# The first search of a gathered layer in two parts, one head after the other

## The chip, the cores and the metric

The kernel runs on one core of one Trainium2 chip. The core has five engines with a queue each: TensorE (PE, matrix products), VectorE (DVE), ScalarE (ACT), GpSimd (POOL) and SyncE (SP), and 16 DMA engines that move data between HBM and the on-chip memory SBUF. PE writes to PSUM. The metric is the device time of one execution in microseconds (us), the median of several.

## What is computed

A model of several layers on 256 tokens of 1024 numbers each, all in float32. The part that matters here is the second kind of feed-forward layer, which occurs twice (stages `peer0` and `peer1`). Each token picks 16 experts for each of 8 heads out of 16384 by product keys, and every expert is one row of `u` and one of `v`:

```python
def peer_ffn(h, w_q, sub_keys, u, v):
    q = (ht @ w_q).reshape(T, PEER_HEADS, 2, PEER_QDIM // 2)
    s = jnp.einsum('thpd,pnd->thpn', q, sub_keys)
    top_s, top_i = lax.top_k(s, PEER_TOPK)
    cand_s = top_s[:, :, 0, :, None] + top_s[:, :, 1, None, :]
    cand_i = top_i[:, :, 0, :, None] * PEER_NKEYS + top_i[:, :, 1, None, :]
    best_s, best_j = lax.top_k(cand_s.reshape(T, PEER_HEADS, -1), PEER_TOPK)
    experts = jnp.take_along_axis(cand_i.reshape(T, PEER_HEADS, -1), best_j, axis=-1)
    gates = jax.nn.softmax(best_s, axis=-1)
    act = jax.nn.gelu(jnp.einsum('cd,ced->ce', xc, u[ec]))
    return jnp.einsum('ce,ced->cd', gc * act, v[ec])
```

## The kernel before

**Gathers.** The 256 tokens lie in two tiles of 128, and 8 heads by 16 picks make 128 picks a token, so a layer needs 256 gathers. Gather m fetches for each of 128 tokens the row of u and v of its pick m: 128 rows of 8 KB, 1.05 MB. POOL issues them in order of m (line 686) into a ring of 8 slots (`RING`). Gather m from 8 on first waits until PE has used the slot of m - 8 (`v_used`), and each unit of 32 gathers (`UNIT`) waits for its picks (`experts_made`). A unit is two heads of one tile.

**What is done with a gather.** DVE makes a dot product of the u rows with the tokens (line 1982). For every two gathers (`BATCH`) ACT makes the gelu (line 943), DVE makes two diagonal matrices from gelu and gate (`weights`, line 1971), and PE weighs the v rows with them (`weigh`, line 1427), which frees the slot.

**Before the first gather.** The queries are h times w_q, in four groups of 512 columns (four query blocks of 128, that is two heads). Group 0 is projected at once (`project`, line 987), ACT copies it from PSUM (`take`, line 743), PE scores it against the keys (`key_scores`, line 1387), ACT copies the scores (`copy_keys`, line 917), and DVE searches the two heads (`search(0)`): sixteen largest of 128 for each of four query blocks (lines 1861 to 1877), the 256 sums of each head (1887), sixteen largest of those (1894 to 1910), and the expert numbers from them (1915 to 1944). Then the gates (lines 1948 to 1959, with an exponential on ACT, line 923). Meanwhile PE turns the tokens back to rows (`turn_tok`, line 1376, copied by `copy_tok`, line 910), projects group 1 at once and makes its scores. Only then is PE ready to weigh, and ACT, whose queue holds `take` of group 1, `take_row` and `copy_keys(1)` ahead of the first gelu, ready for that. Groups 2 and 3 are projected between the weighings, two products behind each of gathers 0 to 15 and 26 to 41 (`project_step`, line 1400). The search of each later unit is spread over the gathers of the unit before it, one step behind each dot product from the fourth on.

**Order.** Each engine runs its own queue in the order written, and semaphores tie them. SP loads the weight groups into three slots, each when the group three before it has been projected (line 521): the last w_q group behind projection 0, the odd layer's weights behind the later projections. Nothing else moves while the gathers run.

## Time and profile before

| | us |
|---|---|
| median of 3 runs | 2480.36 |
| lowest and highest | 2479.7 and 2483.38 |
| the profiled execution, its own time | 2479.74 |
| its span | 2477.9 |
| PE busy | 1919.7 (77%) |
| DVE busy | 1354.5 (55%) |
| POOL busy | 552.8 (22%) |
| ACT busy | 323.3 (13%) |

The profile is of one execution. Times in the rows are counted from the start of its span. The first gathered layer runs from about 883 us to 1580, the second from 1770 to the end. In a timeline row the numbers are the start and the duration of a group of like instructions, and the brackets give the idle time of the engine before it and who ended it. PE has two records for each product of 256 or 512 columns, so `x64` is 32 products. PEld is PE's loading of the stationary operand. DMA share is the mean busy share of the 16 DMA engines.

### The profile page before, as it was taken

To read this page: it belongs to the slowest core of one execution; us is meant where nothing else is said; L and a number is where in the kernel's file an instruction comes from.
4 is the path that set the end of the run, shared out by engine and by line. 5 is a ranking of instruction groups with operands and counts; after the bars stand their busy time and mean duration, and the time that the engine had idled before them with its cause. 6 is when DMAs were issued, how large, how long until landed. Compare 5 with 4: busy or idle time off the path is not lost. (4 is left out here: it accounts for less than half of the span.)

```text
span 2477.9 us, 24089 instructions
## 1 busy us (share of the span) xinstructions
PE 1919.7 (77%) x8926; PEld 1027.1 (41%) x8926; DVE 1354.5 (55%) x3221; ACT 323.3 (13%) x795; POOL 552.8 (22%) x563
## 2 busy tenths in 40 slices
PE   6998666666589688977777777788889877777776
PEld 4666333333266464532222222374565322232222
DVE  2623000010167537767877786555177788678765
ACT  1052000000111321000000000203211100000000
POOL 1000000000000004344343433100034434444432
PEclk9998888888789799999999999999999999999999
DMA  9987999999698039999999999693289999999997
GB/s 381 409 259 289 428 428 431 430 428 429 282 374 327 11 124 419 419 419 421 421 415 421 413 420 421 272 370 115 81 328 421 421 421 421 412 414 421 414 422 292
DMA packets 145523, 894.76 MB, mean 361 GB/s; under 512 B 17305, under 2 KB 29433, under 8 KB 62457
## 3 DMA queue, kind: packets, MB, share of 16 engines
q0 software_dynamic: 73728, 536.90, 52.3%
q1 hardware_dynamic: 71672, 356.25, 36.1%
q8 instruction: 75, 1.23, 0.2%
q14 instruction: 48, 0.39, 0.0%
HBM read 889.68 MB, written 3.42 MB: 360 GB/s over the span
## 5 line engine op out<-in xcount | busy, mean ns | idle before, releaser
L1427 PE MATMUL psum<-sb_area 128*128 128x512 f32 x2048 | 974.4, 619 | 286.3 <-DVE sb_area L1971 283.5
L1982 DVE CUSTOM_DVE_ANT_0 sb_area<-sb_area 128x1024 f32<-128x1024 f32 x512 | 627.2, 1225 | 305.3 <-DMA sb_area<-in_peer_uv,sb_peer_e 303.2
L686 POOL DMA_INDIRECT sb_area<-in_peer_uv,sb_peer_e x512 | 542.2, 1059 | 1123.0 <-PE psum L1427 721.7
L1427 PEld LDWEIGHTS psum<-sb_area 128*128 128x128 f32 x2048 | 382.6, 195 | 835.1 <-DVE sb_area L1971 454.1
L1171 PE MATMUL psum<-sb_area 128*32 128x256 f32 x2048 | 173.6, 514 | 134.4 <-DMA sb_area<-in_moe_w_gu 132.4
L987 PE MATMUL psum<-sb_area 128*128 128x256 f32 x1040 | 235.1, 388 | 5.1 <-ACT sb_area L730 3.5
L1626 DVE COPY sb_area<-psum 128x128 f32<-128x128 f32 x32 | 9.3, 292 | 397.0 <-PE psum L1181 397.0
L987 PEld LDWEIGHTS psum<-sb_area 128*128 128x128 f32 x1040 | 202.0, 195 | 39.1 <-issue 5.1
L943 ACT ACTIVATE sb_small<-sb_small 128x2 f32<-128x2 f32 x256 | 52.1, 204 | 1201.7 <-DVE sb_small L1982 1201.7
L1971 DVE SCALAR_TENSOR_TENSOR sb_area<-sb_ident,sb_small,sb_area 128x128 f32<-128x128 f32 x512 | 156.1, 346 | 44.9 <-ACT sb_small L943 40.4
L1171 PEld LDWEIGHTS psum<-sb_area 128*32 128x32 f32 x2048 | 83.5, 146 | 224.2 <-DMA sb_area<-in_moe_w_gu 145.9
L992 PE MATMUL psum<-sb_area 128*128 128x512 f32 (+1 forms) x392 | 165.2, 581 | 11.9 <-DVE sb_area L1839 10.3
L1540 DVE SCALAR_TENSOR_TENSOR sb_area<-sb_area,sb_c_silu 128x2048 f32<-128x2048 f32 x56 | 131.7, 2351 | 74.6 <-DMA sb_area<-in_ada_w 71.5
L674 POOL TENSOR_SCALAR_AFFINE_SELECT sb_area<-sb_area 128x256 f32<-128x256 f32 x1 | 0.4, 408 | 767.0 <-DVE sb_area L1808 767.0
L992 PEld LDWEIGHTS psum<-sb_area 128*128 128x128 f32 x392 | 74.4, 192 | 98.7 <-issue 84.8
L1400 PE MATMUL psum<-sb_area 128*128 128x256 f32 x256 | 66.6, 383 | 0.0
L1194 PE MATMUL psum<-sb_area 128*32 128x256 f32 x1024 | 61.9, 381 | 4.6 <-DVE sb_area L1626 4.6
L1400 PEld LDWEIGHTS psum<-sb_area 128*128 128x128 f32 x256 | 49.1, 193 | 33.9 <-issue 30.5
L1514 DVE TENSOR_TENSOR sb_area<-psum,sb_row 128x512 f32<-128x512 f32 x12 | 8.3, 692 | 79.7 <-PE psum L992 79.7
L806 ACT ACTIVATE sb_area<-psum 128x128 f32<-128x128 f32 x32 | 8.9, 278 | 294.6 <-PE psum L1171 294.6
L1016 PE MATMUL psum<-sb_ident,sb_area 128*128 128x128 f32 x96 | 19.9, 393 | 34.9 <-DVE sb_area L1488 34.9
L743 ACT ACTIVATE sb_area<-psum 128x1024 f32<-128x1024 f32 x21 | 21.4, 1021 | 188.9 <-PE psum L987 188.9
(276 smaller groups left out, 1331.6 us busy)
## 6 DMA issues: line engine op xcount, KB each, us to landing
sb_area<-in_moe_w_gu SPq DMA_DIRECT2D x32, 4096.0 KB, 33.8
sb_area<-in_ada_w SPq DMA_DIRECT2D x72, 1024.0 KB, 12.9
sb_area<-in_moe_w_dn SPq DMA_DIRECT2D x32, 2048.0 KB, 24.4
sb_area<-in_peer_w_q SPq DMA_DIRECT2D x8, 2048.0 KB, 8.1
sb_area<-in_sb_w_in SPq DMA_DIRECT2D x6, 2048.0 KB, 21.7
sb_area<-in_odd_w_in SPq DMA_DIRECT2D x6, 2048.0 KB, 13.2
sb_area<-in_even_w_in SPq DMA_DIRECT2D x5, 2048.0 KB, 17.9
sb_area<-in_peer_uv,sb_peer_e POOLq DMA_INDIRECT x512, 13.0
```

The costliest lines, as they stand in the source:

```text
L686: pool.indirect_dma_start(uv_rows[s], None, rows, bass.IndirectOffsetOnAxis(ap=peer_e[:, m:m + 1], axis=0)).then_inc(named(f"uv_loaded{s}" ...
L743: act.activation(g["dst"], src, ACT.Copy, scale=g["scale"]).then_inc(proj_out, 1)
L943: act.activation(gelu[:, cols], dots[:, cols], ACT.Gelu_apprx_tanh).then_inc(named("gelu_done"), 1)
L987: last = pe.matmul(ps[:, b + f // 2, (f % 2) * T:(f % 2 + 1) * T], w[:, k, f * P:(f + 1) * P], src[:, k, :], start=(k == 0), stop=(k == nk ...
L992: last = pe.matmul(ps[:, b + t, 0:cols], src[:, k, t * P:(t + 1) * P], w[:, k, 0:cols], start=(k == 0), stop=(k == nk - 1))
L1171: last = pe.matmul(ps[SLOTS * q:SLOTS * (q + 1), 6 + e % 2, 0:2 * FQ], xe[e // QUAD % 2][:, k, SLOTS * (e % QUAD):SLOTS * (e % QUAD + 1)], ...
L1194: last = pe.matmul(ps[SLOTS * q:SLOTS * (q + 1), 6 + b, 0:DQ], turned_act[b][:, SLOTS * f:SLOTS * (f + 1)], moe_dn[e % EXPERT_BUFS][:, f, ...
L1400: last = pe.matmul(ps[:, b + f // 2, (f % 2) * T:(f % 2 + 1) * T], wring[n % 3][:, k, f * P:(f + 1) * P], hT[:, k, :], start=(k == 0), sto ...
L1427: last = pe.matmul(ps[:, 4 + 2 * t + half, :], diag[:, s, :], uv_rows[s][:, D + half * HALF:D + (half + 1) * HALF], start=(k == 0), stop=( ...
L1540: dve.scalar_tensor_tensor(acc, ring[slot], c, acc, ALU.mult, ALU.add).then_inc(ada_used, 1)
L1971: last = dve.scalar_tensor_tensor(diag[:, m % RING, :], ident[:, :], gelu[:, m % BODY:m % BODY + 1], g.broadcast_to([P, P]), ALU.mult, ALU ...
L1982: dve.tensor_tensor_reduce(uv_rows[s][:, 0:D], uv_rows[s][:, 0:D], h_tok[:, m // P, :], 1.0, 0.0, ALU.mult, ALU.add, dots[:, m % BODY:m % ...
```

## The change

The first unit of each gathered layer is split by head. PE makes the first two query blocks of group 0 (16 products), signals `head_projected`, makes three products of the third block, scores the first head on token tile 0, turns part of the tokens, and then makes the other 13 products and the scores of the second head. ACT copies the first two blocks and the first head's scores on their own, and the rest behind them. DVE runs the search for head 0 alone, then for head 1, and makes the gates of both behind that. POOL starts gather 0 when head 0's picks are there, and waits once more before gather 16 (`PEER_K`). All counts of the semaphores `keys_copied`, `key_scored` and `experts_made` get one more a layer. Later units are searched as before, two heads at a time. In the diff the rest of `find_picks` only replaces the fixed sizes by `count`, `nq` and `nk`.

```diff
@@ -441,6 +441,16 @@
 
         def layer_of(stage):
             return int(stage[-1])
+
+        KEY_PARTS = 2 * NT * 2 + 1
+
+        def keys_at(L, i, t):
+
+            return KEY_PARTS * L + NT * i + t + 2
+
+        def experts_at(L, m):
+
+            return (UNITS + 1) * L + (m // UNIT + 2 if m >= UNIT else m // PEER_K + 1)
         block = ctx.enter_context(nc.Block())
         ADA = [(I["ada_w"][0], 0), (I["ada_w_2"][0], KC), (I["ada_w_2"][1], KC)]
         BIAS_AT = [(0, 64), (1, 0), (1, 48)]
@@ -679,8 +689,8 @@
                 rows = I["peer_uv_2"].rearrange("l e d -> (l e) d")
                 for m in range(T):
                     s = m % RING
-                    if m % UNIT == 0:
-                        pool.wait_ge(named("experts_made"), UNITS * L + m // UNIT + 1)
+                    if m % UNIT == 0 or m == PEER_K:
+                        pool.wait_ge(named("experts_made"), experts_at(L, m))
                     if L * T + m >= RING:
                         pool.wait_ge(named("v_used"), L * T + m - RING + 1)
                     pool.indirect_dma_start(uv_rows[s], None, rows, bass.IndirectOffsetOnAxis(ap=peer_e[:, m:m + 1], axis=0)
@@ -913,7 +923,11 @@
                 def copy_keys(i):
 
                     for t in range(NT):
-                        act.wait_ge(named("key_scored"), NT * (4 * L + i) + t + 1)
+                        act.wait_ge(named("key_scored"), keys_at(L, i, t))
+                        if (i, t) == (0, 0):
+                            act.activation(key_score[:, 2:GQ, :].rearrange("p q n -> p (q n)"), ps[:, 6, 2 * P:4 * P],
+                                           ACT.Copy).then_inc(named("keys_copied"), 1)
+                            continue
                         act.activation(key_score[:, t * HP + GQ * i:t * HP + GQ * (i + 1), :].rearrange("p q n -> p (q n)"), ps[:, 6 + t, :],
                                        ACT.Copy).then_inc(named("keys_copied"), 1)
 
@@ -922,8 +936,16 @@
                     act.wait_ge(named("gate_diff"), UNITS * L + u + 1)
                     act.activation(gate[:, heads, :], gate[:, heads, :], ACT.Exp).then_inc(named("gate_exp"), 1)
 
-                take(*groups_here[0])
+                n, g = groups_here[0]
+                b = 2 * (n % 2)
+                act.wait_ge(named("head_projected"), L + 1)
+                act.activation(g["dst"][:, 0:2, :], ps[:, b, :].rearrange("p (f t) -> p f t", t=T), ACT.Copy).then_inc(named("head_out"), 1)
+                act.wait_ge(named("key_scored"), keys_at(L, 0, 0) - 1)
+                act.activation(key_score[:, 0:2, :].rearrange("p q n -> p (q n)"), ps[:, 6, 0:2 * P],
+                               ACT.Copy).then_inc(named("keys_copied"), 1)
                 copy_tok(0)
+                act.wait_ge(proj_done, n + 1)
+                act.activation(g["dst"][:, 2:4, :], ps[:, b + 1, :].rearrange("p (f t) -> p f t", t=T), ACT.Copy).then_inc(proj_out, 1)
                 copy_tok(1)
                 copy_keys(0)
                 copy_tok(2)
@@ -1377,12 +1399,18 @@
                                             ident[:, :])
                     last.then_inc(named("ht_psum"), 1)
 
-                def key_scores(i, t):
-
-                    pe.wait_ge(proj_out, groups_here[i][0] + 1)
+                def key_scores(i, t, part=range(GQ)):
+
+                    if part == range(2):
+                        pe.wait_ge(named("head_out"), L + 1)
+                        pe.wait_ge(named("keysT_ready"), L + 1)
+                    else:
+                        pe.wait_ge(proj_out, groups_here[i][0] + 1)
+                    if part == range(2, GQ):
+                        pe.wait_ge(named("keys_copied"), keys_at(L, 0, 0) - 1)
                     if i:
-                        pe.wait_ge(named("keys_copied"), NT * (4 * L + i - 1) + t + 1)
-                    for j in range(GQ):
+                        pe.wait_ge(named("keys_copied"), keys_at(L, i - 1, t))
+                    for j in part:
                         q = GQ * i + j
                         last = pe.matmul(ps[:, 6 + t, j * P:(j + 1) * P], qkT[:, q, t * P:(t + 1) * P],
                                          keysT[:, q % 2, :], start=True, stop=True)
@@ -1402,12 +1430,28 @@
                     if at == 2 * KC - 1:
                         last.then_inc(proj_done, 1)
 
-                project(*groups_here[0])
-                pe.wait_ge(named("keysT_ready"), L + 1)
+                n, _ = groups_here[0]
+                bank = 2 * (n % 2)
+                pe.wait_ge(w_loaded[n % 3], w_turns(n))
+                pe.wait_ge(proj_out, n - 1)
+
+                def head_products(f, ks):
+
+                    for k in ks:
+                        last = pe.matmul(ps[:, bank + f // 2, (f % 2) * T:(f % 2 + 1) * T], wring[n % 3][:, k, f * P:(f + 1) * P],
+                                         hT[:, k, :], start=(k == 0), stop=(k == KC - 1), skip_group_check=True)
+                    return last
+
+                head_products(0, range(KC))
+                head_products(1, range(KC)).then_inc(named("head_projected"), 1)
+                head_products(2, range(3))
+                key_scores(0, 0, range(2))
                 turn_tok(0)
+                head_products(2, range(3, KC))
+                head_products(3, range(KC)).then_inc(proj_done, 1)
                 turn_tok(1)
-                for t in range(NT):
-                    key_scores(0, t)
+                key_scores(0, 0, range(2, GQ))
+                key_scores(0, 1)
                 turn_tok(2)
                 turn_tok(3)
                 pe.wait_ge(named("h_tok_ready"), 4 * (L + 2))
-                def search(u):
+                def find_picks(u, first_head, count):
 
 
                     t, i = u // 4, u % 4
-                    dve.wait_ge(named("keys_copied"), NT * (4 * L + i) + t + 1)
-                    rows = [(t * HP + GQ * i + j, key_score[:, t * HP + GQ * i + j, :], key_left[:, j, :]) for j in range(GQ)]
+                    half = count < GH
+                    dve.wait_ge(named("keys_copied"), keys_at(L, i, t) - (1 if half and first_head == 0 else 0))
+                    at = t * HP + GQ * i + 2 * first_head
+                    nq, nk = 2 * count, count * PEER_K
+                    rows = [(at + j, key_score[:, at + j, :], key_left[:, j, :]) for j in range(nq)]
...
+                    square = [P, count, PEER_K, PEER_K]
+                    first = slice(at, at + nq, 2)
+                    second = slice(at + 1, at + nq, 2)
+                    mine = slice(at, at + nq)
...
+                    top = t * PEER_HEADS + GH * i + first_head
+                    heads = [(top + h, cand[:, h, :], cand_left[:, h, :]) for h in range(count)]
...
-                        last = dve.tensor_reduce(pick[:, u, :], hits[:, :, :], AX_X, ALU.add)
+                        last = dve.tensor_reduce(pick[:, u, picks], hits, AX_X, ALU.add)
...
-                    dve.tensor_scalar(peer_e[:, u * GK:(u + 1) * GK], pick_e, float(L * PEER_EXPERTS), None, ALU.add
+                    dve.tensor_scalar(peer_e[:, u * GK + picks.start:u * GK + picks.stop], pick_e[:, 0:nk], float(L * PEER_EXPERTS), None, ALU.add
                                       ).then_inc(named("experts_made"), 1)
+
+                def gates(u):
+
                     mine = slice(u * GH, (u + 1) * GH)
...
+                def search(u):
+
+                    yield from find_picks(u, 0, GH)
+                    yield from gates(u)
...
-                for _ in search(0):
+                for head in range(GH):
+                    for _ in find_picks(0, head, 1):
+                        pass
+                for _ in gates(0):
                     pass
                 others = iter(())
                 dve.wait_ge(named("h_tok_ready"), 4 * (L + 2))
```

## Rows read from the trace of the kernel before

**Rows 1.** The page: DMA share in 40 slices, and the gathers' queue.
```profile
DMA  9987999999698039999999999693289999999997
...
q0 software_dynamic: 73728, 536.90, 52.3%
```

**Rows 2.** Windows: length, busy PE, PEld, DVE, ACT, POOL, clock, DMA share, GB/s.
```profile
916.00:920.00 4.00, 4.00 (x20) 3.54 (x19) 3.83 (x16) 0.00 (x0) 0.00 (x0) 1.00 0.00 0
...
1200.00:1300.00 100.00, 77.42 (x162) 30.17 (x161) 79.66 (x221) 6.87 (x23) 44.13 (x40) 0.97 1.01 417
```

**Rows 3.** The gathers' line L686: whom POOL waited for, us and times.
```profile
  DVE sb_peer_e L1944: 379.4, 2
```

**Rows 4.** Timeline, first gathered layer, projection 0 to search, and projection 1.
```profile
890.49 15.17 PE L987 MATMUL psum<-sb_area 128*128 128x256 f32 x64
...
905.70 1.02 ACT L743 ACTIVATE sb_area<-psum 128x1024 f32<-128x1024 f32 x1 [14.58 <-PE psum L987]
...
906.78 2.05 PE L1387 MATMUL psum<-sb_area 128*128 128x128 f32 x16 [0.24 <-ACT sb_area L743]
...
907.98 0.60 ACT L917 ACTIVATE sb_area<-psum 128x512 f32<-128x512 f32 x1 [0.27 <-PE psum L1387]
...
908.61 0.87 DVE L1861 MAX8 sb_area<-sb_area 128x8 f32<-128x128 f32 x4 [19.64 <-ACT sb_area L917]
...
910.50 14.08 PE L987 MATMUL psum<-sb_area 128*128 128x256 f32 x64 [0.79 <-ACT sb_area L910]
```

**Rows 5.** Timeline, the search of unit 0 and the first gather.
```profile
914.63 0.76 DVE L1894 MAX8 sb_area<-sb_area 128x8 f32<-128x256 f32 x2
...
921.56 1.28 DVE L1937 TENSOR_REDUCE sb_area<-sb_area 128x32 f32<-128x512 bf16 x2
...
923.11 0.18 DVE L1944 TENSOR_SCALAR sb_peer_e<-sb_area 128x32 uint32<-128x32 f32 x1
...
923.58 1.14 POOL L686 DMA_INDIRECT sb_area<-in_peer_uv,sb_peer_e  x1 [139.47 <-DVE sb_peer_e L1944]
```

**Rows 6.** Timeline, from the gelu's table to the ninth gather.
```profile
928.80 1.28 ACT L943 ACT_TABLE_LOAD   x1
...
929.50 1.22 DVE L1982 CUSTOM_DVE_ANT_0 sb_area<-sb_area 128x1024 f32<-128x1024 f32 x1 [5.21 <-DMA sb_area<-in_peer_uv,sb_peer_e]
...
933.59 0.20 ACT L943 ACTIVATE sb_small<-sb_small 128x2 f32<-128x2 f32 x1 [3.50 <-DVE sb_small L1982]
...
934.49 3.78 PE L1427 MATMUL psum<-sb_area 128*128 128x512 f32 x4 [5.48 <-DVE sb_area L1971]
...
938.55 0.93 POOL L686 DMA_INDIRECT sb_area<-in_peer_uv,sb_peer_e  x1 [4.19 <-PE psum L1427]
```

**Rows 7.** Timeline, a weighing at full clock and the issues behind it.
```profile
942.81 1.88 PE L1427 MATMUL psum<-sb_area 128*128 128x512 f32 x4
...
944.97 0.94 POOL L686 DMA_INDIRECT sb_area<-in_peer_uv,sb_peer_e  x1 [0.65 <-PE psum L1427]
...
947.55 0.94 POOL L686 DMA_INDIRECT sb_area<-in_peer_uv,sb_peer_e  x1 [1.65 <-PE psum L1427]
```

**Rows 8.** Timeline: dot 18; then of the second layer the gelu's table, dots 4, 16, 24.
```profile
975.71 1.23 DVE L1982 CUSTOM_DVE_ANT_0 sb_area<-sb_area 128x1024 f32<-128x1024 f32 x1 [0.36 <-DMA sb_area<-in_peer_uv,sb_peer_e]
...
1816.16 1.28 ACT L943 ACT_TABLE_LOAD   x1
...
1828.51 1.23 DVE L1982 CUSTOM_DVE_ANT_0 sb_area<-sb_area 128x1024 f32<-128x1024 f32 x1 [0.37 <-DMA sb_area<-in_peer_uv,sb_peer_e]
...
1858.32 1.23 DVE L1982 CUSTOM_DVE_ANT_0 sb_area<-sb_area 128x1024 f32<-128x1024 f32 x1
...
1878.41 1.23 DVE L1982 CUSTOM_DVE_ANT_0 sb_area<-sb_area 128x1024 f32<-128x1024 f32 x1 [0.37 <-DMA sb_area<-in_peer_uv,sb_peer_e]
```

**Rows 9.** Windows, as in rows 2: the clock after a pause, and with short pauses.
```profile
933.00:934.00 1.00, 0.00 (x0) 0.00 (x0) 0.73 (x3) 0.20 (x1) 0.92 (x1) 0.93 1.04 434
...
996.00:1000.00 4.00, 2.04 (x11) 1.35 (x10) 1.85 (x4) 0.20 (x1) 0.94 (x1) 1.00 1.03 415
```

More of the change, by code:

```diff
@@ L1891, in search @@
                     marked()
-                    heads = [(t * PEER_HEADS + GH * i + h, cand[:, h, :], cand_left[:, h, :]) for h in range(GH)]
+                    top = t * PEER_HEADS + GH * i + first_head
+                    heads = [(top + h, cand[:, h, :], cand_left[:, h, :]) for h in range(count)]
                     for r, s, _ in heads:
@@ L1913, in search @@
                     marked()
-                    flat = best_at[:, t * PEER_HEADS + GH * i:t * PEER_HEADS + GH * (i + 1), :].rearrange("p h k -> p (h k)")
-                    dve.tensor_scalar(best_hi, flat, 4, None, ALU.logical_shift_right)
-                    mark(dve.tensor_scalar(best_lo, flat, PEER_K - 1, None, ALU.bitwise_and))
+                    flat = best_at[:, top:top + count, :].rearrange("p h k -> p (h k)")
+                    dve.tensor_scalar(best_hi[:, 0:nk], flat, 4, None, ALU.logical_shift_right)
+                    mark(dve.tensor_scalar(best_lo[:, 0:nk], flat, PEER_K - 1, None, ALU.bitwise_and))
                     marked()
-                    dve.tensor_copy(best_row, best_hi)
-                    mark(dve.tensor_copy(best_col, best_lo))
+                    dve.tensor_copy(best_row[:, 0:nk], best_hi[:, 0:nk])
+                    mark(dve.tensor_copy(best_col[:, 0:nk], best_lo[:, 0:nk]))
                     yield
                     marked()
-                    sides = [(match[0], best_row, first, pick_i), (match[1], best_col, second, pick_j)]
+                    sides = [(match[0][:, 0:nk, :], best_row[:, 0:nk], first, pick_i), (match[1][:, 0:nk, :], best_col[:, 0:nk], second, pick_j)]
+                    picks = slice(first_head * PEER_K, first_head * PEER_K + nk)
                     for hits, place, _, _ in sides:
-                        last = dve.tensor_tensor(hits[:, :, :], iota_16[:, :].unsqueeze(1).broadcast_to([P, GK, PEER_K]),
-                                                 place.unsqueeze(2).broadcast_to([P, GK, PEER_K]), ALU.is_equal)
+                        last = dve.tensor_tensor(hits, iota_16[:, :].unsqueeze(1).broadcast_to([P, nk, PEER_K]),
+                                                 place.unsqueeze(2).broadcast_to([P, nk, PEER_K]), ALU.is_equal)
                     mark(last)
```

12 lines of the change are left out of this document (4 added, 8 removed).

## The prediction

> **What bounds the kernel now.** I read the slices of the span first. In the two long stretches at its middle and end, the 16 DMA engines are at nine tenths or more, and the q0 row says what they carry: 537 MB, the 512 gathers of 1.05 MB each [rows 1]. A window in the middle of a stretch shows 417 GB/s at a DMA share of 1.01, while PE and DVE are busy under 80 of 100 us [rows 2]. So once a gathered layer runs, its time is bytes: from the dot product of gather 4 to that of gather 24 of the second layer, both begun the moment the data landed, 49.90 us pass for 20 gathers, **2.49 us each** [rows 8]. What isn't bytes is the stretch before. Between 916 and 920 us DMA moves nothing [rows 2], and POOL waits 379 us in all, in two waits, for DVE to write the first picks [rows 3]. Then I read the timeline of that stretch, to see what fixes the first gather and what fixes the ninth, which needs a ring slot back.
>
> **What the change moves: the first gather.** Before, the 32 weight products of group 0 (64 records) take 15.17 us from 890.49, the copy 1.02, the scores start at 906.78, their copy ends at 908.58, and DVE starts at 908.61 [rows 4]. After, DVE needs only the first 16 products. The clock is low at first (a record of projection 1, all at full speed, takes 14.08 / 64 = 0.22 us [rows 4]; 15.17 us hold 64 of them with about 2.4 us at half speed, which give 5.6 records, and 58.4 at some 0.217), so record 32 ends at 892.9 + 26.4 x 0.217 = 898.6. The copy of 512 columns (0.60 us, the score copy's row [rows 4]) hides under the three products put behind it (6 x 0.217 = 1.3 us, to 899.9). Two score products are a quarter of the 2.05 us for eight, 0.5 us, plus 0.2 us hand-over, and the copy of 256 columns about 0.4 us: DVE starts at 901.0, 7.6 us earlier. The search of two heads lasts 908.61 to 923.29 [rows 4, 5]. For one head the counts halve (four MAX8 of 0.22 us to two) or the elements do (two reductions of 512 elements take 1.28 us; MAX8 takes 0.22 us for 128 elements and 0.38 for 256, 1.25 ns an element, so 256 fewer are worth 0.32 of 0.64), while the small ones of 0.18 us and the hand-overs of 0.03 to 0.04 stay: about 1.7 us fixed, half of the other 13, so **8.3 us** [rows 5]. Picks at 909.4, first gather at **909.7 instead of 923.58, 13.9 us earlier**. The second head's picks follow at 917.7; gather 16 needs them, no earlier than 909.7 + 16 x 1.25 = 930. Nobody waits there. The added cost on DVE, some 2 us of small operations and the doubled hand-overs, lies in time when DVE had nothing.
>
> **What sets the ninth gather.** The ring has eight slots. A head start beyond them is worth nothing unless PE frees slot 0, and PE needs ACT's gelu, which is behind take(group 1), take_row and copy_keys(1) in ACT's queue. None of these gets earlier. PE does the same products before group 1 as before; the new waits add a bubble of some 0.2 us where the second part's scores wait for the second copy, and ACT copies the keys in three pieces, not two. I take PE and ACT **0.15 us later**, with 0 and 0.7 as ends (the longer is one more score copy, 0.60, with its hand-over). Before, ACT has its table for the gelu at 930.08 but must wait for dot product 1 until 933.59, and PE starts to weigh 0.90 us behind the gelu [rows 6]. After, the first eight gathers landed long ago, so the table sets it: 930.08 + 0.15 + 0.9 = **PE at 931.1 instead of 934.49**. The clock matters too. Before, PE stood still from 929.0; the granted clock fell in the window 933 to 934 and the first weighing took 3.78 us [rows 6, 9]. After, PE stands still 2.1 us; the windows with PE half idle between products keep 1.00 [rows 9], so I take full speed: 1.88 us [rows 7]. A slot is gathered into again 2.16 us after PE started on it (942.81 to 944.97 [rows 7]). So the ninth gather is issued at 931.1 + 2.16 = 933.3 instead of 938.55. The eight before it are through by about 933: the first lands 5.9 us behind its issue (923.58 to 929.50 [rows 5, 6]), at 915.6, and 7 x 2.49 makes 933.0; the last w_q group, 2 MB, may push it by up to 5 us, in time that would be idle anyway. The ninth lands at 939.2 and so moves from 936.7: DMA idles for 3 to 4 us. **This is where part of the head start is lost.**
>
> **The next sixteen.** Up to gather 15 PE weighs a gather and does a step of projection 2, 2.58 us together, against DMA's 2.49 (POOL's issues behind PE stand at 944.97 and 947.55 [rows 7]). Before, a queue of issued gathers covers this. After, the queue is empty, so DMA runs at PE's pace: gather 23 is issued at 933.3 + 15 x 2.58 = 972.0 and lands 5.9 later, 977.9; then PE, without projection steps, takes at most 1.88 a gather and is faster than DMA, and gather 24 lands at 980.4. Before: gather 18's dot starts on landing at 975.71 [rows 8], and 6 x 2.49 more give 990.6. **Gain 10.2 us.** The load of the odd layer's weights that PE sets off behind step 15 costs both the same bytes. In the second layer the table is there at 1816.16 + 1.28 = 1817.44, PE starts at 1818.5, gather 23 is issued at 1820.65 + 38.7 = 1859.35 and gather 24 lands at 1867.7, against 1878.4 before [rows 8]: **gain 10.7 us**. DVE must keep up meanwhile: twelve gathers with their share of the next search took 1858.32 - 1828.51 = 29.81 us, 2.48 each [rows 8], under 2.58. Behind gather 24 DMA is full again and each layer is only shifted; what follows starts on its last gather.
>
> **Sum.** 10.2 + 10.7 = 20.9 us off the profiled execution's 2479.74 us (its span of 2477.9 and 1.8 around it, which the change doesn't touch) gives 2458.8. The median of the runs is 0.6 us above that execution: **2459.5 us**.
>
> **A rule of the skill, weighed.** A gather's issue row is 0.94 us when nothing holds it, and 1.14 with the first one here [rows 5, 7]. The Trainium skill (SBUF — State Buffer, "SBUF: two separate sides") says that GpSimd can't write descriptors while VectorE holds their shared port with certain operations, and that speaks against issuing beside a search. By that rule the first eight issues come at up to 2.2 us each; by the rows at 1.25. Either is faster than DMA's 2.49, so the sum stays as it is.
>
> **Rivals.**
> (a) *The whole head start is kept*: DMA never idles behind gather 7. That gives 2 x 13.9 = 27.8 us, 2452.6. Against it stands ACT's table row, which no edit moves [rows 6]. 6%.
> (b) *PE falls to the low clock before weighing all the same*, as it does now. The first two weighings then take up to 942.81 - 934.49 = 8.3 instead of 5.2 us [rows 6, 7]: 3.2 us less in each layer, 2465.8. The pause of 2.1 us speaks against it. 13%.
> (c) *DVE becomes the bound of gathers 4 to 21*: it enters them with no slack in the queue. At 2.9 us instead of 2.58 it would lose 18 x 0.32 = 6 us a layer, 2471. The 2.48 us measured speak against it. 6%.
> (d) *Nothing comes of it*: the head start only fills the ring, and PE, late by the upper bound and at the low clock, frees it about when it does now. Within 5 us of before. 5%.
> (e) *Slower*: the new waits in group 0 (first copy, second copy, keys copied) hold PE so long that its clock falls and projection 1 runs at half speed, 14 us more. Then PE weighs at 945, the ninth gather lands some 3 us later than it does now, and each layer loses 3 to 4 us: 2487. It decides once the ninth issue is over 10 us behind my 933.3, at 943.5. The three products laid under the first copy speak against it: I find no bubble over 0.3 us. 5%.
>
> **How the numbers follow.** Forecast 65%, with its own range 2454 to 2464 (landing 5.6 or 7 us, PE late by 0 to 0.7, clock). The range takes in (a) and (b): 2452 to 2468, which leaves out 16% ((c), (d) and (e)). A measurement of this kernel tells about 0.2%, 5 us, from no change. Faster by more than that: 65 + 6 + 13 + 6 = 90%; within: 5%; slower: 5%.
>
> **What would show it.** First gather 13 to 15 us earlier against the start of projection 0; DVE's MAX8 7 to 8 us earlier; PE's first weighing 3 us earlier and at 1.9 us; a DMA gap of about 3 us between gathers 7 and 8; issues 2.58 us apart up to gather 23; from gather 24 on the old pace of 2.49. It is wrong if PE's first weighing isn't earlier, if gathers 8 to 24 land more than 2.6 us apart, or if the shift at gather 24 isn't there at the layer's last.

## The result, and the profile after

The changed kernel takes 2465.26 us (median of 4 runs, 2462.86 to 2466.98) against 2480.08 us for the kernel before in runs beside it (4 runs). The ratio is 0.9942, 95% interval 0.9929 to 0.9954: 0.58% faster, 14.8 us. In a second series it gave 0.9943. The forecast was 2459.5 us, a gain of 20.9: the direction and the mechanism were right and the time is inside the range, but the gain is a third smaller than forecast. The profiled execution took 2466.98 us (span 2465.2), 12.8 us less than the one of before.

The page first: the DMA share in 40 slices and the gathers' queue (packets, MB, share of 16 engines), to set beside [rows 1].

```profile
DMA  9987999999798049999999999693299999999996
...
q0 software_dynamic: 73728, 536.90, 52.8%
```

The bytes are the same 537 MB. The two long stretches at nine tenths are still there; what moved is when the first of them starts. Whom POOL waited for at the gathers' line (us, times):

```profile
  PE psum L1471: 730.0, 464
  DVE sb_peer_e L1993: 355.3, 2
```

It waits 24.1 us less for first picks than in [rows 3]. About that much head start arrived at the first gathers, and half of it at the end. The timeline of the first gathered layer shows the way there (start us, length us, engine, line, operation; in brackets the idle time before it and what ended it):

```profile
890.32 11.16 PE L1441 MATMUL psum<-sb_area 128*128 128x256 f32 x38
...
902.37 0.49 DVE L1908 MAX8 sb_area<-sb_area 128x8 f32<-128x128 f32 x2 [13.58 <-ACT sb_area L944]
...
911.51 1.14 POOL L696 DMA_INDIRECT sb_area<-in_peer_uv,sb_peer_e  x1 [127.46 <-DVE sb_peer_e L1993]
...
911.93 14.08 PE L1009 MATMUL psum<-sb_area 128*128 128x256 f32 x64 [0.79 <-ACT sb_area L920]
...
930.23 1.28 ACT L965 ACT_TABLE_LOAD   x1
...
932.43 2.75 PE L1471 MATMUL psum<-sb_area 128*128 128x512 f32 x4 [1.99 <-DVE sb_area L2028]
...
935.46 0.94 POOL L696 DMA_INDIRECT sb_area<-in_peer_uv,sb_peer_e  x1 [13.92 <-PE psum L1471]
```

Against [rows 4, 5]: DVE's first MAX8 now takes two blocks, not four, and comes 6.2 us earlier; the first gather comes 12.1 us earlier. Then projection 1 starts 1.4 us *later*, the table 1.4 us later, and the ninth gather only 3.1 us earlier [rows 6]. The second gathered layer does the same at the full clock (the first gather, the first weighing, the ninth gather, gather 23, and the dot product of gather 24, which began when its data landed):

```profile
1793.47 0.94 POOL L696 DMA_INDIRECT sb_area<-in_peer_uv,sb_peer_e  x1 [227.85 <-DVE sb_peer_e L1993]
...
1814.42 1.98 PE L1471 MATMUL psum<-sb_area 128*128 128x512 f32 x4 [1.99 <-DVE sb_area L2028]
...
1816.67 0.94 POOL L696 DMA_INDIRECT sb_area<-in_peer_uv,sb_peer_e  x1 [13.55 <-PE psum L1471]
...
1855.37 0.94 POOL L696 DMA_INDIRECT sb_area<-in_peer_uv,sb_peer_e  x1 [1.64 <-PE psum L1471]
...
1865.94 1.23 DVE L2042 CUSTOM_DVE_ANT_0 sb_area<-sb_area 128x1024 f32<-128x1024 f32 x1 [0.31 <-DMA sb_area<-in_peer_uv,sb_peer_e]
```

And the windows behind the ninth issue in the first layer (columns as in [rows 2]), where DMA has little to do, and then moves less than its 417 to 422 GB/s for a long time:

```profile
933.00:934.00 1.00, 1.00 (x3) 0.38 (x2) 1.00 (x3) 0.00 (x0) 0.00 (x0) 0.75 1.06 429
934.00:936.00 2.00, 2.00 (x5) 1.18 (x4) 1.73 (x5) 0.20 (x1) 0.54 (x1) 0.50 0.79 247
936.00:940.00 4.00, 4.00 (x13) 2.52 (x12) 4.00 (x20) 0.20 (x1) 1.33 (x2) 0.88 0.75 249
940.00:944.00 4.00, 4.00 (x13) 2.20 (x13) 4.00 (x14) 0.00 (x0) 1.66 (x1) 1.00 0.90 295
...
952.00:956.00 4.00, 4.00 (x14) 2.33 (x13) 4.00 (x10) 0.20 (x1) 1.73 (x2) 1.00 0.98 360
...
960.00:964.00 4.00, 4.00 (x13) 2.20 (x13) 3.99 (x10) 0.20 (x1) 2.92 (x2) 1.00 1.01 348
```

Absolute times are a poor measure between executions: the layer itself starts at other times in each (its first transposes at 885.37 us before, 885.11 here, 887.41 in "again", another execution of the same kernel). So all that follows is counted from the layer's first transposes. In the table are us from there for the kernel before, and for every other kernel how much earlier the same event comes; "gather 24" and "last" are starts of the dot products of gather 24 and of the layer's last gather. One profiled execution each, and it is not always near the median: 2463.63 us against 2458.55 for "warm", 2459.17 against 2455.35 for "inter", and 2453.61 against 2461.5 for "steps_later", the shortest of its five.

| kernel | layer 1: first gather | ninth | gather 24 | last | layer 2: first gather | ninth | gather 24 | last | ratio of times, 95% |
|---|---|---|---|---|---|---|---|---|---|
| before (us) | 38.2 | 53.2 | 108.4 | 698.4 | 38.2 | 52.8 | 105.7 | 689.2 | 1 |
| changed | 11.8 | 2.8 | 2.8 | 4.2 | 13.5 | 4.9 | 8.5 | 8.8 | 0.9942 (0.9929 to 0.9954) |
| again | 14.7 | 5.2 | 8.8 | 7.3 | 13.5 | 4.9 | 8.0 | 8.9 | 0.9943 (0.9924 to 0.9962) |
| late | 3.1 | 2.8 | 2.3 | 2.1 | 4.8 | 4.9 | 5.0 | 5.1 | 0.9967 (0.9956 to 0.9979) |
| inter | 13.5 | 13.4 | 14.5 | 10.9 | 12.4 | 11.6 | 11.6 | 11.0 | 0.9905 (0.9888 to 0.9922) |
| warm | 15.4 | 7.2 | 9.4 | 9.2 | 15.4 | 6.8 | 11.1 | 9.9 | 0.9915 (0.9897 to 0.9932) |
| inter_whole | 0.0 | -0.4 | 0.1 | -3.1 | -0.1 | -1.1 | -3.0 | -2.7 | 1.0018 (1.0007 to 1.0029) |
| inter_warm | 15.4 | 14.6 | 16.7 | 12.8 | 15.4 | 14.6 | 13.1 | 13.6 | 0.9887 (0.9866 to 0.9908) |
| before_warm | 1.9 | 2.7 | 1.4 | 1.5 | 1.9 | 2.0 | 2.6 | 1.3 | 0.9972 (0.9961 to 0.9984) |
| quiet | 12.6 | 4.4 | 6.9 | 6.2 | 12.8 | 4.2 | 7.8 | 8.2 | 0.9943 (0.9927 to 0.9960) |
| steps_later | 13.5 | 3.9 | 11.9 | 6.8 | 14.5 | 5.9 | 10.6 | 11.7 | 0.9928 (0.9914 to 0.9941) |

The first gather came 12 to 15 us earlier, as forecast. The ninth kept 3 to 5 us of it, and the last 4 to 9. The two "last" columns of the changed kernel add up to 13.0 us; the two profiled executions differ by 12.8.

One column needs care. In the first layer the transfers of the odd layer's weights run beside gathers 20 to 27 or so, which then land 3.2 to 3.3 us apart instead of 2.5. Before the change and in most kernels they begin ahead of gather 24 (at 980.0 us before; gather 24's dot product starts at 993.7). In "inter", "inter_whole", "inter_warm" and "steps_later" they begin behind it (in "steps_later" at 980.5, with gather 24's at 976.2). So about 3.1 us of these four kernels' 14.5, 0.1, 16.7 and 11.9 in "gather 24" of layer 1 is only this load moved back; it is paid by the layer's last gather.

### The profile page after: what moved, and what is told of

Same layout as the page of the kernel before. It is cut to its first block and busy times, and to the rows that moved or that the text cites. A ratio compares the mean times of both kernels' runs of the same rounds, so it can differ in the third digit from the quotient of the medians.

```text
span 2465.2 us, 24127 instructions
## 1 busy us (share of the span) xinstructions
PE 1921.0 (78%) x8926; PEld 1027.6 (42%) x8926; DVE 1358.2 (55%) x3249; ACT 324.2 (13%) x799; POOL 556.9 (23%) x563
## 3 DMA queue, kind: packets, MB, share of 16 engines
q0 software_dynamic: 73728, 536.90, 52.8%
## 5 line engine op out<-in xcount | busy, mean ns | idle before, releaser
L1471 PEld LDWEIGHTS psum<-sb_area 128*128 128x128 f32 x2048 | 383.9, 195 | 819.5 <-DVE sb_area L2028 433.8
L1009 PE MATMUL psum<-sb_area 128*128 128x256 f32 x912 | 203.5, 385 | 5.1 <-ACT sb_area L740 3.5
L1009 PEld LDWEIGHTS psum<-sb_area 128*128 128x128 f32 x912 | 175.1, 193 | 34.8 <-issue 5.1
L1193 PEld LDWEIGHTS psum<-sb_area 128*32 128x32 f32 x2048 | 82.7, 146 | 225.8 <-DMA sb_area<-in_moe_w_gu 147.8
L1014 PE MATMUL psum<-sb_area 128*128 128x512 f32 (+1 forms) x392 | 166.5, 585 | 11.9 <-DVE sb_area L1883 10.3
L1014 PEld LDWEIGHTS psum<-sb_area 128*128 128x128 f32 x392 | 75.4, 194 | 99.0 <-issue 84.7
L1428 PE MATMUL psum<-sb_area 128*128 128x256 f32 x256 | 66.6, 383 | 0.0
L1428 PEld LDWEIGHTS psum<-sb_area 128*128 128x128 f32 x256 | 49.1, 192 | 33.6 <-issue 30.2
L1216 PEld LDWEIGHTS psum<-sb_area 128*32 128x32 f32 x1024 | 33.4, 109 | 23.7 <-issue 8.4
## 6 DMA issues: line engine op xcount, KB each, us to landing
sb_area<-in_moe_w_dn SPq DMA_DIRECT2D x32, 2048.0 KB, 24.1
```

The source lines that it names most:

```text
L1009: last = pe.matmul(ps[:, b + f // 2, (f % 2) * T:(f % 2 + 1) * T], w[:, k, f * P:(f + 1) * P], src[:, k, :], start=(k == 0), stop=(k == nk ...
L1014: last = pe.matmul(ps[:, b + t, 0:cols], src[:, k, t * P:(t + 1) * P], w[:, k, 0:cols], start=(k == 0), stop=(k == nk - 1))
L1193: last = pe.matmul(ps[SLOTS * q:SLOTS * (q + 1), 6 + e % 2, 0:2 * FQ], xe[e // QUAD % 2][:, k, SLOTS * (e % QUAD):SLOTS * (e % QUAD + 1)], ...
L1216: last = pe.matmul(ps[SLOTS * q:SLOTS * (q + 1), 6 + b, 0:DQ], turned_act[b][:, SLOTS * f:SLOTS * (f + 1)], moe_dn[e % EXPERT_BUFS][:, f, ...
L1428: last = pe.matmul(ps[:, b + f // 2, (f % 2) * T:(f % 2 + 1) * T], wring[n % 3][:, k, f * P:(f + 1) * P], hT[:, k, :], start=(k == 0), sto ...
L1471: last = pe.matmul(ps[:, 4 + 2 * t + half, :], diag[:, s, :], uv_rows[s][:, D + half * HALF:D + (half + 1) * HALF], start=(k == 0), stop=( ...
```

## The experiments

**The change once more, and without its point.** Theory A: the time is the start of the gathers, cut down by what the ring and TensorE let through. "again" is the changed kernel unedited. "late" keeps the split into two heads, but gather 0 waits until the picks of both are written:

```
-            return (UNITS + 1) * L + (m // UNIT + 2 if m >= UNIT else m // PEER_K + 1)
+            return (UNITS + 1) * L + m // UNIT + 2
...
-                    if m % UNIT == 0 or m == PEER_K:
+                    if m % UNIT == 0:
```

> The changed kernel once more, for a closer ratio and a second trace. In its first trace the two layers gained 4.3 and 8.6 us, and the first layer lost about 3 us of that because TensorE stood at the low clock for 3 us longer in projection 0 and fell to it again at the first weighing. If that is a matter of the moment at which the clock is looked at, this trace shows another pair of gains, between 4 and 9 us each, with the low stretches at other places, and the time scatters by 2 us. If it belongs to the change, the first layer again gains about 4 us and the second about 8.5. Time 2463 to 2467 either way.

> The changed kernel, but POOL waits for the picks of both heads before gather 0; everything else is as in the change. The gathers start some 8.7 us later. Theory A: the ninth gather is set by PE's first weighing (the ring of eight), so the first eight only fill the ring and most of their head start is idle time later. Then the ninth is issued at the same time as in the changed kernel, the eight before it land 2 to 8 us later, the queue is never empty, landings come 2.49 us apart through gathers 8 to 24 instead of about 3, and the time is that of the changed kernel within 3 us (2463 to 2468). Theory B: the early start itself is what the change gains. Then 8.7 us a layer are lost and the time is 2479 to 2482, as before the change.

"again" took 2464.47 us, "late" 2471.53. In "again" the layers gained 7.3 and 8.9 us instead of 4.2 and 8.8: the small gain of the first layer belongs to the first profiled execution and not to the change, as the first of the two expectations had it. Late met neither expectation: 7 us slower than the change, but 9 us faster than before. The rows show why. With all picks awaited, the first gather still comes 3.1 and 4.8 us earlier than before, because the first head's search runs while the second head's products are still computed; the DMA engines are saturated from then on, and the last gather of each layer is just that much earlier (2.1 and 5.1). So more than half of the change's gain (9 of 16 us) is search begun earlier, and the rest is gathers issued before the second search. What the early gathers are worth later on is seen where the ninth is issued at the same time. In the first layer "late" and the changed kernel issue gather 8 within 0.1 us of each other (50.42 and 50.35 us behind the transposes), and gather 23 too (89.98 and 89.97); the changed kernel has started its gathers 8.8 us sooner. The same stretch in "late":

```profile
936.00:944.00 8.00, 8.00 (x24) 4.69 (x24) 6.71 (x31) 0.41 (x2) 2.93 (x3) 0.95 1.03 413
944.00:952.00 8.00, 8.00 (x27) 4.79 (x26) 8.00 (x27) 0.41 (x2) 4.93 (x4) 1.00 1.02 415
952.00:960.00 8.00, 8.00 (x27) 4.79 (x26) 7.93 (x26) 0.20 (x1) 3.07 (x4) 1.00 1.01 422
```

and in the changed kernel:

```profile
936.00:944.00 8.00, 8.00 (x25) 4.72 (x24) 8.00 (x33) 0.20 (x1) 3.00 (x3) 0.94 0.83 272
944.00:952.00 8.00, 8.00 (x27) 4.79 (x26) 8.00 (x30) 0.41 (x2) 3.21 (x4) 1.00 0.99 377
952.00:960.00 8.00, 8.00 (x27) 4.79 (x26) 7.87 (x24) 0.41 (x2) 3.59 (x4) 1.00 0.97 375
```

PE does the same work in both. DMA moves 413 to 422 GB/s with a queue in hand and 272 to 377 without one. Gather 8 landed 6.2 us earlier in the changed kernel (56.67 against 62.91), gather 19 only 0.2 us earlier (90.15 against 90.31): in this execution of that layer the whole head start beyond the ninth issue was gone. In "again" it was not: there gather 24 came 6.5 us earlier than in "late". The second layer is the steadier case. Gather 8 is again issued at the same time in both (47.90 and 47.89), gather 7 landed 8.8 us earlier in the changed kernel (49.66 against 58.45), gather 8 7.2 us, gather 19 4.0 and gather 24 3.5 us earlier. The same 30 us there, in the changed kernel and in "late":

```profile
1820.00:1850.00 30.00, 30.00 (x94) 17.48 (x93) 29.80 (x97) 1.42 (x7) 13.18 (x12) 1.00 0.99 387
...
1820.00:1850.00 30.00, 28.82 (x90) 16.66 (x89) 27.72 (x93) 1.22 (x6) 12.88 (x12) 1.00 1.01 422
```

The traces hold each DMA packet too. Of the gathers' 8 KB packets in these 30 us, 93 of 1416 took more than 0.4 us in the changed kernel (the longest 1.6), and none of 1545 in "late" (the longest 0.33); the middle one took 0.31 us in both. The loss is in single slow packets, not in a lower pace of all.

**TensorE freed earlier.** "inter" lays 4 of the 16 steps of projection 1, and the four key scores, behind the first weighings instead of ahead of them, moves ACT's copies accordingly, and puts everything planned behind it a few gathers later:

```
-PROJECT_AT = {2: 0, 3: 26}
...
+PROJECT_AT = {2: 6, 3: 32}
...
+STEPS_AHEAD = 12
...
-                project(*groups_here[1])
...
+                for at in range(STEPS_AHEAD):
+                    project_step(1, at)
...
                     weigh(m)
+                    if m < 2 * KC - STEPS_AHEAD:
+                        project_step(1, STEPS_AHEAD + m)
+                    elif m < 2 * KC - STEPS_AHEAD + NT:
+                        key_scores(1, m - 2 * KC + STEPS_AHEAD)
```

> The changed kernel with PE freed earlier: the row of gates (make_row) comes first, 12 of the 16 steps of projection 1 run ahead of the first weighing and the last 4 behind gathers 0 to 3, scores of group 1 behind gathers 4 and 5, the later projections six gathers later, the searches four gathers later in their unit. Theory A (the head start is lost because PE frees the ring's first slot late): the first weighing starts at about 924.5 us instead of 932.4 in the first layer, the ninth gather is issued while gathers 5 to 7 are still in flight, DMA never idles, and gather 8 lands 10 us (first layer) and 13 us (second) earlier than in the kernel before; these gains stay to the layer's end: 2480 - 23 = 2457, some 8 to 10 us under the changed kernel. Theory B (something else, DMA's own rate beside the search, takes the head start): the landings of gathers 8 to 24 stay about 3 us apart although the ring is refilled early, and the time stays at 2463 to 2467.

It took 2455.35 us, 9 us less than the change. The first weighing and the issues behind it:

```profile
925.28 1.96 PE L1473 MATMUL psum<-sb_area 128*128 128x512 f32 x4
...
927.51 0.93 POOL L697 DMA_INDIRECT sb_area<-in_peer_uv,sb_peer_e  x1 [5.06 <-PE psum L1473]
...
930.09 0.93 POOL L697 DMA_INDIRECT sb_area<-in_peer_uv,sb_peer_e  x1 [1.65 <-PE psum L1473]
```

The ninth gather follows the first at 15.1 us instead of 24, before the first eight have landed, and the issues keep the same 2.58 us of spacing. So a pace of 2.58 costs little as long as a queue stands ahead of it. The last gather is 11 us earlier in both layers. But this edit alters two things, so it was also applied to the kernel before.

> The kernel before, with only the order of projection 1 changed: its steps lie between the first six weighings and between the search groups, so that TensorE comes to the next unit's work earlier; the first unit's search stays whole (both heads' picks before gather 0). Theory A (what the change gains is the start of the gathers; the interleaving gained in the earlier run only because the head split had opened a gap behind gather 7 that it closes): the first gather stays 38.2 us behind the layer's first transposes, within 0.5, the DMA engines stay saturated from it on, gather 24 lands at 108.4 and 105.6 us, and the time is 2478 to 2482. Theory B (the freeing of TensorE is a gain of its own, whatever the first gather does): 9 us less, near 2471.

"inter_whole" took 2483.63 us, even slower than before by 0.18%. Where the picks come late, TensorE ready earlier buys nothing: the first gather is where it was (38.2), and the ninth comes 0.4 and 1.1 us later. The steps put off are then paid with the queue that had been built up. In one stretch of the second layer DMA falls to 333 GB/s, and DVE waits 3.08 us for one gather:

```profile
1876.00:1884.00 8.00, 8.00 (x26) 4.66 (x25) 4.08 (x13) 0.41 (x2) 4.65 (x4) 1.00 0.92 333
...
1881.84 1.22 DVE L1988 CUSTOM_DVE_ANT_0 sb_area<-sb_area 128x1024 f32<-128x1024 f32 x1 [3.08 <-DMA sb_area<-in_peer_uv,sb_peer_e]
```

The head split and the interleaving need each other: 15 us and -3 us alone, 25 us together.

**The clock.** "warm" adds small products that PE does while it would wait: 15 ahead of the layer's transposes, 5 behind them, and two of 512 columns in the 2 us before the first weighing.

```
+            def fill(count):
+                for _ in range(count):
+                    pe.matmul(ps[:, 7, 0:P], ident[:, :], ident[:, :], start=True, stop=True)
...
+                fill(15)
                 transpose_norm(stage)
+                fill(5)
...
+                for _ in range(2):
+                    pe.matmul(ps[:, 2 * (groups_here[2][0] % 2), :], ident[:, :], hT[:, 0:2, :].rearrange("p k t -> p (k t)"),
+                              start=True, stop=True)
```

> The changed kernel with idle PE time filled by products that nobody reads: 15 small ones before the transposes of the layer's input, 5 behind them, and 2 of 512 columns in the pause before the first weighing. Theory: the low clock costs the changed kernel up to 3 us in projection 0 and 1 to 1.5 us at the first weighing of a layer. With the fillers the granted clock stays 1.00 through both, projection 0's first 32 records take about 7.2 us instead of 9.9 and 8.6, PE weighs 2 to 4 us earlier, and since the ninth gather hangs on that, the time falls by 3 to 6 us to 2459 to 2462. Rival: DMA, not PE, sets the pace by then, and the time stays within 1 us of the changed kernel. If the fillers come too late or are too few, the clock falls all the same and nothing changes.

2458.55 us, 6 us less than the change and about what had been expected. PE's timeline and clock there:

```profile
929.13 1.88 PE L1470 MATMUL psum<-sb_area,sb_ident 128*128 128x512 f32 x4
...
932.15 1.99 PE L1481 MATMUL psum<-sb_area 128*128 128x512 f32 x4 [0.27 <-DVE sb_area L2038]
...
932.00:936.00 4.00, 3.85 (x11) 2.20 (x12) 3.73 (x8) 0.20 (x1) 0.94 (x1) 1.00 1.00 375
```

The first weighing takes 1.99 us instead of 2.75 (3.32 in "again"), and the ninth gather comes 7 us earlier than before in both layers. The same products in the kernel before, and together with "inter":

> The kernel before with the same clock-keeping products and nothing else. Theory A (these products shorten the path from the transposes to the first gather, and the DMA engines are saturated behind it): the first gather comes 2 to 3 us earlier in each layer (35.2 to 36.2 us behind the first transposes), gather 24 as much, and the time is 2474 to 2477. Theory B (their gain in the changed kernel came from the first weighing at the full clock alone, which in the kernel before has slack): no gain, 2479 to 2482.

> The head split with projection 1 interleaved, and in addition small products that keep TensorE's granted clock up ahead of the first unit. Theory A (start of the gathers is what counts, with the queue kept filled): the first gather comes 15.4 us earlier than before in both layers (38.2 to 22.8 us behind the first transposes), against 13.5 and 12.4 without these products, the dies of the queue stay filled, and gather 24 lands 13 to 14 us earlier in each layer: 2451 to 2454. Theory B (the interleaved order already takes all that the DMA queues let through): the same as the interleaved order alone, 2455.4 within 1.

"before_warm" took 2474.16 us: its first gather is 1.9 us earlier (2 to 3 had been expected), and each layer ends 1.3 to 1.5 us earlier. That is 2.8 us in the profile against 6 between the medians; the profiled executions themselves differ by 4.9 us, 1.8 of it ahead of the first layer's transposes, and the rest isn't explained. What the products give the change can be read from the ratios: 0.9915 for "warm" over 0.9972 for "before_warm" is 0.9943, the ratio of the change without them. So as far as these intervals tell (some 3 to 5 us to either side), a kernel whose clock is kept up gains by the change as much as one whose clock isn't. The medians give no sign that the clock is why the gain fell short of the forecast. "inter_warm" took 2452.59 us, as expected, 1.1% less than before and the shortest median of this study, though its interval overlaps that of "inter": its first gather is 15.4 us earlier and its last 12.8 and 13.6.

**Is VectorE's search in the way?** In the changed kernel the next unit's search runs beside gathers 4 to 11, just when the queue is short. "quiet" starts it eight gathers later.

```
-SEARCH_AT = 4
-EXP_AT = 22
+SEARCH_AT = 12
+EXP_AT = 30
```

> The changed kernel with the planned place of the next unit's search and exponentials put later (search from slot 12, exponential at 30), so that VectorE does not search beside gathers 4 to 11. Theory C (VectorE's search beside the issues makes the landings slow while few gathers are in flight): in both layers gathers 8 to 12 land 2.5 to 2.6 us apart and gather 8 lands within 7 us of its issue; gather 24 lands 2 to 4 us earlier a layer, 2457 to 2461. Theory D (the slow landings belong to a short queue, whatever VectorE does): landings of gathers 8 to 19 are 2.75 to 3.05 us apart as in the changed kernel, with single steps of 3.6 us or more, and the time is within 2.5 of 2464.5.

2465.07 us: no difference from the change. The first layer's dots 9 to 12, with no search beside them:

```profile
941.79 1.23 DVE L2042 CUSTOM_DVE_ANT_0 sb_area<-sb_area 128x1024 f32<-128x1024 f32 x1 [0.87 <-DMA sb_area<-in_peer_uv,sb_peer_e]
944.36 1.23 DVE L2042 CUSTOM_DVE_ANT_0 sb_area<-sb_area 128x1024 f32<-128x1024 f32 x1 [0.45 <-DMA sb_area<-in_peer_uv,sb_peer_e]
948.12 1.23 DVE L2042 CUSTOM_DVE_ANT_0 sb_area<-sb_area 128x1024 f32<-128x1024 f32 x1 [2.53 <-DMA sb_area<-in_peer_uv,sb_peer_e]
950.69 1.23 DVE L2042 CUSTOM_DVE_ANT_0 sb_area<-sb_area 128x1024 f32<-128x1024 f32 x1 [0.45 <-DMA sb_area<-in_peer_uv,sb_peer_e]
```

Two of the three steps are normal (2.57 us), and one is 3.76 us, with DVE idle for 2.53 us of it. From dot 9 to dot 19 the mean step is 2.73 us in both layers. Long steps exist without any search beside them, so theory C falls: the search isn't their cause. Nor is the length of the issue rows: in the second layer of the changed kernel gather 11 landed 4.3 us behind gather 10, and the issue rows of gathers 8 to 13 took 0.94 us each. What the cause is stays open.

**TensorE's pace.** "steps_later" keeps projection 1 whole and ahead of the weighings, and puts the steps of projection 2, the copies and projection 3 six gathers later, and the next unit's search and exponentials four later ("quiet" had shown that the place of the search alone changes nothing). The first six weighings then have no step between them.

```
-SEARCH_AT = 4
-EXP_AT = 22
-PROJECT_AT = {2: 0, 3: 26}
...
+SEARCH_AT = 8
+EXP_AT = 26
+PROJECT_AT = {2: 6, 3: 32}
...
```

> The changed kernel with the steps of projection 2 laid beside weighings 6 to 21 instead of 0 to 15 (and the search, the copies and projection 3 six later too); projection 1 stays whole ahead of the weighings. Theory E (the head start is lost because TensorE frees slots only every 2.58 us while the queue is empty): the six issues behind gather 8 come 1.7 to 1.9 us apart instead of 2.58, the queue holds some 4 us more, gathers 9 to 24 land 2.5 to 2.6 us apart, gather 24 comes 3 to 6 us earlier in each layer, and the time is 2456 to 2461. Theory F (the loss is the late ninth issue alone and what a step beside a weighing costs is only put off, as in the interleaved order without the head split, which lost 3 us): gather 24 comes within 1.5 us of the changed kernel's, and the time is 2462 to 2467.

```profile
1805.25 0.94 POOL L696 DMA_INDIRECT sb_area<-in_peer_uv,sb_peer_e  x1 [13.59 <-PE psum L1471]
1806.97 1.07 POOL L696 DMA_INDIRECT sb_area<-in_peer_uv,sb_peer_e  x1 [0.78 <-PE psum L1471]
1808.68 0.94 POOL L696 DMA_INDIRECT sb_area<-in_peer_uv,sb_peer_e  x1 [0.65 <-PE psum L1471]
```

The issues stand 1.72 us apart. In the second layer gathers 9 and 10 still land 3.65 and 3.89 us behind the ones before them, and then gathers 11 to 33 land 2.48 to 2.50 us apart. Gather 24 comes 2.1 us earlier there than in the changed kernel, and the last 2.9. In the first layer gather 24 comes 9.1 or 3.1 us earlier (against "changed" or "again"), but 3.1 us of that is the weights' load moved behind it, and at the last gather the layer gains 6.8 us against 4.2 or 7.3, so nothing is shown there. The trace is of the shortest execution, 2453.61 us, 5.4 us of it ahead of the first layer's transposes; the other four took 2460.75 to 2463.5. The median, 2461.5 us, lies half a microsecond outside what theory E said and outside what F said too. It is 3 to 4 us under the changed kernel's, and the two intervals overlap. E's mechanism, a steady pace once a queue stands, is seen in the second layer's rows; its worth in the time, 3.8 us against 4 to 9, is under what was expected, and not shown beyond the noise.

## Why the prediction came out as it did

**Right.** *The first gather* 13.9 us earlier: 11.8 to 14.7 in the four layers of "changed" and "again". *The search of one head*: its last operation starts 8.67 us behind its first (902.37 to 911.04), forecast 8.3 in all, half a microsecond too little. *The second head's wait costs nobody anything.* *The ring and ACT's queue eat the head start*: a ninth gather 4.9 us earlier in the second layer, at 47.90 us behind the transposes where the forecast's 1820.65 was 47.92. *TensorE's pace of 2.58*: gather 23 issued at 86.60 us in the second layer and forecast at 86.6. Rival (a), the whole head start kept, didn't come, nor did (c), (d) and (e).

**Wrong in size, in the second layer: the landing.** The step said "gather 23 is issued ... and lands 5.9 later", the latency of a gather on an idle queue [rows 5, 6]. It landed 8.1 us later. And "gathers 8 to 24 land more than 2.6 us apart", which the prediction had named as a sign that it is wrong, came true: 2.71 us in the second layer and 3.06 in the first (2.76 and 2.68 in "again"), where the first layer's mean holds four landings beside the weights' load. The source view of gather 23:

```profile
DMA to landing us min/median/max: 8.1/8.1/8.1
```

Those 2.2 us are the whole difference between the forecast gather 24 (94.97 us) and the measured one (97.17), and 1.9 of them are missing at the layer's end (8.8 against 10.7). The step assumed that with the queue empty every gather would land 5.9 us behind its issue and 2.58 behind the last. In fact between gathers 8 and 19 they came 2.77 us apart, because single steps were longer (4.30 us for gather 11, 2.9 to 3.0 for three more), and of a backlog of 2 us, once there, a pace of issues of 2.58 against landings of 2.49 takes off only 0.1 us a gather.

**Wrong in size, in the first layer of the profiled execution: the clock, twice, and the landing more.** "I take PE and ACT 0.15 us later": it was 1.6 us counted from the start of projection 0, since the clock stayed low there longer than before (38 records took 11.16 us; "again" and "warm" have 8.37), and DVE's first MAX8 came 6.2 us earlier instead of 7.6 for the same reason. "I take full speed: 1.88 us" for the first weighing: 2.75 us here and 3.32 in "again", with the granted clock down to 0.50, the lower of TensorE's two levels (1.2 GHz), behind the idle 1.99 us. This is rival (b), to which I gave 13%, in one of the two layers: in the second the same pause of 1.99 us left the clock at 1.00 (1.98 us). That the time of (b), 2465.8, is nearly the measured one is chance: it rests on the clock in both layers, and more than half of what was missing is the landing. In the forecast, the row it was taken from, short pauses at 1.00, was of PE half idle between products [rows 9], and that says nothing of a whole pause of 2 us. Together the two put the ninth issue 2.4 us later than forecast (50.35 against 47.93), but they are a matter of the execution: in "again" 38 records of projection 0 took 8.37 us and the ninth was issued at 48.01, and the filled kernels "warm" and "before_warm" stand 15.6 us apart, as far as the unfilled ones. The first eight landed at 53.1 us instead of 47.6: 2.1 us by the later first gather, 1.9 by its landing (7.8 us behind its issue, with the last w_q group beside it, instead of 5.9) and 1.5 by one long step. Gather 8 landed at 56.67 instead of 53.8, 2.4 us by its issue and 0.4 by its landing. Behind it the landings were 3.04 us apart up to gather 19 (2.55 in "again"). One more term was misread but cancels: "6 x 2.49 more give 990.6" puts gather 24 of the kernel before 3.1 us too early (993.75), because the odd layer's weights, taken there as costing both the same, were left out of both sums. All this gives the layer 4.2 us instead of 10.2; "again" got 7.3.

**The sum.** 10.2 + 10.7 = 20.9 was forecast, 4.2 + 8.8 = 13.0 came in the profiled execution, and 7.3 + 8.9 in another. With the terms as measured in the second layer (ninth gather as forecast, landing 8.1) the same working gives 94.97 + 2.2 = 97.2 and a gain of 8.5. The mechanism held. The term of the sum that was mis-sized in all four layers is the landing: 8.1 and 8.6 us for gather 23 in the two second layers, and 8.6 us for gather 8 in the first layer of "again", where 5.9 was forecast. The clock in the first layer took its part in the one profiled execution, and nothing can be seen of it over the medians. Why single packets are slow behind a short queue stays open. The doubt of the prediction about issuing beside a search is settled too: the first eight issues, seven of them beside the second head's search (911.13 to 919.79), took 0.93 to 1.14 us each and stood 1.24 to 1.45 apart, as in the forecast. (By the rule of the Trainium skill, SBUF — State Buffer, "SBUF: two separate sides", GpSimd could have been held up there; these rows show nothing of it. The longest issue row of the execution is 2.02 us.)

## What to carry to other kernels

A transfer started earlier is only worth what the next resource behind it gives back in time: ask of each ring slot who frees it, and move that work together with the start (15 us alone, 25 us with TensorE's steps interleaved, and a loss of 3 us for the interleaving without the start). A consumer a little slower than the memory (2.58 against 2.49 us) is harmless behind a queue and costly at an empty one, so give it its light steps first and the heavy ones once the queue stands (the rows of "steps_later" point that way, its time alone doesn't prove it). And don't price a queue at its idle latency: take the latency of a row with the same number of transfers ahead of it.

## What the runs showed of the hardware

- **A short gather queue lands late.** Over the profiled executions of before, changed, again, late, inter, warm and steps_later I set each landing step of gathers 9 to 33 (9 to 19 in the first layer) against the time from that gather's issue to the landing of the one before it. With 7 us or more of such work ahead (148 landings) the mean step is 2.5 us and the longest 3.3. With 5 to 7 us (65) it is 2.6 and two are over 3.3; with 4 to 5 us (24) 2.8 and five; under 4 us (15) 3.1 and five. The longest is 4.4 us. A little of the last group is the idle latency alone (5.9 us with 3 us ahead make a step of 2.9); the long steps go beyond it. In windows of 4 us between 944 and 968 us of the changed kernel DMA's share reads 0.92 to 1.02, and its GB/s show the loss (344 to 397 instead of 420): the share counts a slow packet's time as busy. The slow packets are single ones of 0.4 to 1.6 us among others of 0.31. The cause is open. It isn't the search beside it ("quiet"), and nine of the twelve steps over 3.3 us have an issue row of 0.93 to 1.07 us.
- **The granted clock behind a pause of 2 us differs from layer to layer.** The same idle 1.99 us ahead of the first weighing left it at 1.00 in the second layer and was followed by 0.50 (half of 2.4 GHz) in the first; in "again" the window of 4 us there shows 0.57.
- **Executions differ by some us ahead of the stretch that was changed**: the first layer's transposes stand at 885.1 and 887.4 us in two executions of the changed kernel, and at 879.7 in "steps_later", whose edit lies behind them. Two traces are best compared from the layer's own first instruction.
